# Column quarters over accumulated input tiles in the later modulation, and forward transforms from even and odd times, in a diffusion block on one NeuronCore

## The reference, cut to what matters

```
mx = (silu(c) @ ada_w[i] + ada_b[i])          # 6 * 1024 numbers for each layer
sh1x, sc1x, g1x, sh2x, sc2x, g2x = split(mx, 6)

def _fft_conv(u, kern, skip):
    y = irfft(rfft(u, n=512) * rfft(kern)); return y[:, :256] + u * skip
z = x1 * _fft_conv(v, kern[:, 0], skip[0])
y = x2 * _fft_conv(z, kern[:, 1], skip[1])
```

## Time and profile before

| | us |
|---|---|
| median of 3 runs (lowest, highest) | 1964.73 (1961.82, 1973.62) |
| profiled execution, its own time | 1960.14 |
| its span | 1958.2 |
| PE busy | 1776.7 (91% of the span) |
| DVE busy | 773.4 (39%) |
| ACT busy | 531.2 (27%) |
| mean granted clock of TensorE | 0.969 of full speed |

### The profile page before, as it was taken

How to read it: one execution, slowest core, us unless ns; L and a number is a source line. 1 busy time by engine, 2 the same in 40 slices (tenths; PEclk the granted TensorE clock), 3 DMA queues, 4 the chain that set the end, 5 groups by cost and what they waited for, 6 DMA issues and landing times. The chain is left out here.

```text
span 1958.2 us, 34257 instructions
## 1 busy us (share of the span) xinstructions
PE 1776.7 (91%) x13979; PEld 941.9 (48%) x13979; DVE 773.4 (39%) x1910; ACT 531.2 (27%) x993; POOL 52.1 (3%) x45
## 2 busy tenths in 40 slices
PE   5788898898897888999999999898999999999996
PEld 2344555555555544443443443675654444444442
DVE  5766677777777335200100101564735110110101
ACT  3244454554454321111111111213321111111111
POOL 0010000000100000000000001000000000000001
PEclk8989899999999899999999999999999999999998
DMA  9013323323323468999999997232166999999993
GB/s 308 26 33 101 99 73 114 114 77 111 110 76 127 162 238 360 427 428 428 428 429 428 428 416 277 76 128 112 82 272 272 427 428 428 428 428 428 428 413 123
DMA packets 105168, 504.05 MB, mean 257 GB/s; under 512 B 15568, under 2 KB 60352, under 8 KB 79184
## 3 DMA queue, kind: packets, MB, share of 16 engines
q1 hardware_dynamic: 103728, 501.88, 64.4%
q10 hardware_dynamic: 1312, 0.37, 0.1%
HBM read 501.13 MB, written 1.09 MB: 256 GB/s over the span
## 5 line engine op out<-in xcount | busy, mean ns | idle before, releaser
L2009 DVE TENSOR_TENSOR arena<-banks,arena 128x512 f32<-128x512 f32 x32 | 22.1, 692 | 660.5 <-PE banks L1821 660.5
L1821 PE MATMUL banks<-arena 128*64 128x512 f32 x1024 | 226.4, 594 | 10.5 <-DMA arena<-in_moe_w_up 10.5
L1843 PE MATMUL banks<-arena 128*64 128x512 f32 x1024 | 226.8, 596 | 3.3 <-ACT arena L1940 3.3
L1812 PE MATMUL banks<-arena 128*64 128x512 f32 x1024 | 225.3, 593 | 3.3 <-DVE arena L1932 3.3
L775 PE MATMUL banks<-arena 128*128 128x512 f32 (+1 forms) x384 | 159.3, 553 | 0.8 <-ACT arena L1086 0.8
L1821 PEld LDWEIGHTS banks<-arena 128*64 128x64 f32 x1024 | 82.1, 137 | 152.8 <-issue 152.8
L1812 PEld LDWEIGHTS banks<-arena 128*64 128x64 f32 x1024 | 74.2, 137 | 147.8 <-issue 144.2
L1843 PEld LDWEIGHTS banks<-arena 128*64 128x64 f32 x1024 | 70.7, 137 | 154.4 <-issue 150.7
L1934 ACT ACTIVATE arena<-banks,arena 128x128 f32<-128x128 f32 x128 | 48.1, 456 | 335.5 <-PE banks L1801 335.5
L1801 PEld LDWEIGHTS banks<-arena 128*128 128x128 f32 x1024 | 118.4, 194 | 28.1 <-issue 24.3
L1801 PE MATMUL banks<-arena 128*128 128x128 f32 x1024 | 124.5, 281 | 3.5 <-DVE arena L2004 3.5
(11 more groups left out here) (394 smaller groups left out, 2398.0 us busy)
## 6 DMA issues: line engine op xcount, KB each, us to landing
arena<-in_moe_w_gate SPq DMA_DIRECT2D x64, 2048.0 KB, 14.9
arena<-in_moe_w_up SPq DMA_DIRECT2D x64, 2048.0 KB, 17.1
arena<-in_moe_w_down SPq DMA_DIRECT2D x64, 2048.0 KB, 12.8
arena<-in_ada_w SPq DMA_DIRECT2D x128, 192.0 KB, 2.9
arena<-in_ada_w SPq DMA_DIRECT2D x64, 256.0 KB, 3.5
arena<-in_rw_wrkv SPq DMA_DIRECT2D x24, 512.0 KB, 5.1
arena<-in_hy_w_in SPq DMA_DIRECT2D x6, 2048.0 KB, 8.4
arena<-in_ada_w SPq DMA_DIRECT2D x8, 1024.0 KB, 17.0
```

Of the source, the lines that this page charges most:

```text
L1812: mm = pe.matmul(G[j * CAP:(j + 1) * CAP, :], xT[:, t, j * CAP:(j + 1) * CAP], wg[par][j][:, t], start=(t == 0), stop=(t == KT - 1))
L1821: mm = pe.matmul(U[j * CAP:(j + 1) * CAP, :], xT[:, t, j * CAP:(j + 1) * CAP], wu[j][:, t], start=(t == 0), stop=(t == KT - 1))
L1843: mm = pe.matmul(bank[j * CAP:(j + 1) * CAP, :], hT[:, t, j * CAP:(j + 1) * CAP], wd[j][:, t, half * 512:(half + 1) * 512], start=(t == 0) ...
L2009: dve.tensor_tensor(h, U[:, :], sg, ALU.mult).then_inc(h_ready, 1)
```

## The change

It has two parts.

**Later modulation.** A step now cuts the columns into four quarters (128 or 96 columns, `part`). Each 32-partition quarter of the bank takes one quarter of the columns, and the four input tiles are accumulated in PSUM: 16 matmuls in place of four. No sum across quarters is needed: `total`, its matmul, its bank uses `t0` to `t2`, its ACT copy and its ACT-issued DMA go. DVE's additions are as wide as a quarter; the second one writes `row` directly, after a wait for the row's last DMA. SP issues the store (`store`), ahead of the next piece's bias and weights. The bias is loaded as four rows.

**Convolutions.** Each of the four products of one transform becomes one product without accumulation: even times and odd times, real and imaginary, four matmuls in place of eight. ACT copies the two even ones to `half_even`, which lies in the old `half_b`. DVE forms sum and difference, two instructions for each part, and then multiplies as before, with `half_a` used twice and a drain more. ACT waits for `imag_ready` of the half before.

```
@@ LaterModulation
+    def part(self, piece):
+        return self.width(piece) // 4
+    def store(self, sp, m, piece, open_dve):
+        layer, cols = self.place(m, piece)
+        sp.wait_ge(open_dve, OPEN.taken(m, f"h{2 * piece + 1}")[1])
+        sp.dma_start(self.mods[layer, 0, cols].rearrange("(g n) -> g n", g=4),
+                     self.row[0:P:32, 0:self.part(piece)]).then_inc(self.row_out, 16)
@@ load
             sp.wait_ge(open_done, OPEN.done(*before))
-            if half == 0:
-                sp.wait_ge(open_dve, OPEN.taken(*before)[1])
         if half == 0:
-            sp.dma_start(self.bias[0:1, 0:self.width(piece)], ...)
+            if m or k:
+                self.store(sp, *((m, piece - 1) if piece else (m - 1, self.PIECES - 1)), open_dve)
+            sp.dma_start(self.bias[0:P:32, 0:self.part(piece)], ...)
@@ products
-        for g in range(self.HALF):
-            mm = pe.matmul(bank[g * 32:(g + 1) * 32, 0:self.width(piece)], self.cond[:, half * self.HALF + g],
-                           self.w[g][:, 0:self.width(piece)], start=True, stop=True, tile_position=(0, g * 32))
+        n = self.part(piece)
+        for t in range(self.HALF):
+            for g in range(4):
+                mm = pe.matmul(bank[g * 32:(g + 1) * 32, 0:n], self.cond[:, half * self.HALF + t],
+                               self.w[t][:, g * n:(g + 1) * n], start=(t == 0), stop=(t == self.HALF - 1), tile_position=(0, g * 32))
-    def total(self, pe, m, piece, bank): ...
@@ open_order
-        order += [(m, u) for u in ("h1", "t0") if chain]
+        order += [(m, u) for u in ("h1",) if chain]
-        order += [(m, u) for u in ("t1",) if chain]
-        order += [(m, u) for u in ("t2",) if chain]
@@ rwkv_heads, SP, after the rounds
+            later.store(sp, CH - 1, later.PIECES - 1, open_dve)
@@ rwkv_heads, PE and ACT: total(m, 0), total(m, 1), total(m, 2) removed; ACT's last wait for row_out removed
@@ rwkv_heads, DVE, modulate
+                dve.drain()
                 if later_half:
-                    dve.drain()
-                    dve.tensor_tensor(later.acc[:, 0:width], bank[:, 0:width], later.acc[:, 0:width], ALU.add)
+                    if m or piece:
+                        dve.wait_ge(later.row_out, 16 * (later.PIECES * m + piece))
+                    dve.tensor_tensor(later.row[:, 0:n], bank[:, 0:n], later.acc[:, 0:n], ALU.add)
                 else:
-                    if m or piece:
-                        dve.wait_ge(open_done, OPEN.done(*((m, f"t{piece - 1}") if piece else (m - 1, "t2"))))
@@ hyena_convolutions, PE
-                    for n in range(4):
-                        part, ft = n // 2, n % 2
+                    for part in range(2):
                         if od or half:
-                            pe.wait_ge(vhat_ready, (od * 2 + half) * 4 + n - 3)
+                            pe.wait_ge(vhat_ready, (od * 2 + half - 1) * 2 + part + 1)
                         for i in range(TT):
-                            mm = pe.matmul(s.psum[4 + n][:, :], fwd[part][:, i, ft * P:(ft + 1) * P], vt[...], start=(i == 0), stop=(i == TT - 1))
-                        mm.then_inc(dft_done, 1)
+                            pe.matmul(s.psum[4 + part * 2 + i][:, :], fwd[part][:, i, 0:P], vt[...], start=True, stop=True).then_inc(dft_done, 1)
@@ hyena_convolutions, ACT
-                        act.activation(vhat[:, part, ft, c], s.psum[4 + n][:, :], ACT.Copy).then_inc(vhat_ready, 1)
+                    for part in range(2):
+                        act.wait_ge(dft_done, (od * 2 + half) * 4 + part * 2 + 1)
+                        if od or half:
+                            act.wait_ge(imag_ready, od * 2 + half)
+                        act.activation(half_even[part], s.psum[4 + part * 2][:, :], ACT.Copy).then_inc(half_ready, 1)
@@ hyena_convolutions, DVE
+                    for part in range(2):
+                        dve.wait_ge(half_ready, (od * 2 + half) * 2 + part + 1)
+                        dve.wait_ge(dft_done, (od * 2 + half) * 4 + part * 2 + 2)
+                        a, b = half_even[part], s.psum[5 + part * 2][:, :]
+                        dve.tensor_tensor(vhat[:, part, 0, c], a, b, ALU.add)
+                        first, second = ((a, b), (b, a))[part]
+                        dve.tensor_tensor(vhat[:, part, 1, c], first, second, ALU.subtract).then_inc(vhat_ready, 1)
+                    dve.drain()
...
                     dve.tensor_tensor(prod[:, 1, :, c], vhat[:, 0, :, c], khat[:, od, 1, :, c], ALU.mult)
-                    dve.tensor_tensor(half_b, vhat[:, 1, :, c], khat[:, od, 0, :, c], ALU.mult)
                     dve.drain()
-                    dve.tensor_tensor(prod[:, 1, :, c], prod[:, 1, :, c], half_b, ALU.add).then_inc(imag_ready, 1)
+                    dve.tensor_tensor(half_a, vhat[:, 1, :, c], khat[:, od, 0, :, c], ALU.mult)
+                    dve.drain()
+                    dve.tensor_tensor(prod[:, 1, :, c], prod[:, 1, :, c], half_a, ALU.add).then_inc(imag_ready, 1)
```

More of the change, by code:

```diff
@@ L206, in __init__ @@
         self.w = [s.take(512) for _ in range(self.HALF)]
-        self.acc, self.bias, self.row = s.take(512), s.take(512), s.take(512)
+        self.acc, self.bias, self.row = s.take(P), s.take(P), s.take(P)
         self.w_in, self.bias_in, self.row_out = (s.sem(n) for n in ("later_w_in", "later_b_in", "later_out"))
@@ L798, in modulate @@
                 later.products(pe, m, k, open_bank(m, f"h{k}")).then_inc(open_done, 1)
-            def total(m, piece):
-                bank = open_bank(m, f"t{piece}")
-                pe.wait_ge(open_dve, OPEN.taken(m, f"h{2 * piece + 1}")[1])
-                later.total(pe, m, piece, bank).then_inc(open_done, 1)
             def sum_directions(n):
@@ L1006, in _ @@
                     if chain and slot == 8:
-                        total(m, 0)
                         level_two(m, 1)
@@ L1026, in _ @@
                         from_values_early(n)
-                    if chain and slot == 15:
-                        total(m, 1)
                     if early and 15 <= slot < 18:
@@ L1054, in _ @@
                         level_two(n, 0)
-                    if chain and slot == 23:
-                        total(m, 2)
                     if m == CH - 1 and slot >= 9:
@@ L1187, in chain_solve @@
                 act.activation(U, s.psum[7][:, 0:P], ACT.Copy).then_inc(us_ready, 1)
-            def total(m, piece):
-                width = later.width(piece)
-                bank = read(m, f"t{piece}")
-                if m or piece:
-                    act.wait_ge(later.row_out, 16 * (later.PIECES * m + piece))
-                act.activation(later.row[0:1, 0:width], bank[0:1, 0:width], ACT.Copy).then_inc(open_act, 1)
-                act.wait_ge(open_act, OPEN.taken(m, f"t{piece}")[1])
-                layer, cols = later.place(m, piece)
-                act.dma_start(mods[layer, 0, cols].unsqueeze(0), later.row[0:1, 0:width]).then_inc(later.row_out, 16)
             for m in ROUNDS:
@@ L1261, in _ @@
                         level_two(n, 0)
-                    if chain and slot == 23:
-                        total(m, 2)
-            act.wait_ge(later.row_out, CH * later.PIECES * 16)
         @block.vector
```

26 lines of the change are left out of this document (10 added, 16 removed).

## The result

| | before | after |
|---|---|---|
| median of 4 runs each (lowest, highest) | 1967.86 (1961.82, 1973.62) | 1943.36 (1939.95, 1946.65) |
| ratio to before, 95% interval | | 0.9883 [0.9858, 0.9909] |
| profiled execution, own time | 1960.14 | 1943.53 |
| its span | 1958.2 | 1941.3 |
| mean granted clock | 0.969 | 0.963 |

The ratio is worth 23.0 us (18 to 28). The changed kernel was timed a second time, beside other runs: 0.9910 [0.9886, 0.9934], 17.7 us. The change gains about 20 us where 26.2 were forecast, at the lower edge of the forecast's 20 to 32; the forecast of 1936 is 7 us low.

What follows compares the result with a forecast made beforehand. PE was taken as the bound, busy for 91% of the span, with gaps from DVE and weight waits. Heads 22.7 plus convolutions 3.5 gave 26.2 us, so 1936 us, range 1923 to 1950.

Steps and rivals of the forecast that it cites:

- rounds above 71 us: Heads: a sign that the prediction is wrong would be rounds staying above 71 us; rounds near 69 were expected.
- The totals: Heads: 24 totals taken off PE, 0.95 us for each first and 0.74 for each other, 19.4 us altogether.
- the key projection: Heads, between h3 and L775: total removed and DVE's reading of h3 earlier, 1.26 us gained, at worst 0.74.
- The quarter products: Heads, 48 steps of L239: 32 short records instead of eight, no change taken; at worst 0.43 us a step, 21 us.
- The rival built on that estimate: Heads' quarter steps: records are paid one by one, time about 1957, by the page's reading 1963; chance 0.06.
- the one of groups that follow one another: Heads, L239: the four groups don't stand abreast, steps cost 96 us more, time 2030; chance 0.04.
- The sum of the heads: Heads: 3.05 us in each of rounds 0 to 5, 2.4 in round 6, 2.0 in round 7, together 22.7 us.
- My rival of 0.11: Heads: the clock takes gain back, three more rounds pay 4.0 us each; gain 14, time about 1948; chance 0.11.
- The narrow additions: Heads, DVE: h0's shorter addition gives 0.1 us a round; those of h2 and h3 end h3's reading 0.54 us earlier.
- The convolutions: Convolutions: 2.9 us less in the second order, 2.5 in the first, 5.4 together; 3.5 taken, bounds -1 and 7.
- The loss to half clock: Convolutions: a slow transform back behind the new 3.4 us gap costs 1.3 us in each order, 2.6, leaving 2.8.
- The stores on SP: Heads: 24 stores moved to SP, about 0.24 us each to issue, covered, nothing; uncovered 12 us, a rival of 0.03.

Runs made afterwards that it cites:

- mod_only: Kernel before with only the later-modulation part of the change: 1947.45 us, ratio 0.9936 to the kernel before.
- no_totals: Kernel before without the totals, keeping wide products and additions, stores on SP, sum over the four input tiles left out: 1944.09 us, ratio 0.9923.
- no_reload: Changed kernel without loads for each piece's second half; h1, h3, h5 reuse the tiles of h0, h2, h4 (wrong values): 1920.78 us, ratio 0.9779.
- best_b: Changed kernel with the edits of warm_after and even_free, two unused matmuls in the convolutions' gap, h5 at the end of slot 23: 1926.07 us, ratio 0.9810.
- h15_later: Changed kernel with h1 moved from slot 6 to 7 and h5 from slot 21 to the end of slot 23: 1938.60 us, ratio 0.9893.
- warm_before: Kernel before with two unused matmuls a round in the gap ahead of the chain's third step: 1957.82 us, ratio 0.9964.
- conv_only: Kernel before with only the convolutions' part of the change: 1961.42 us, ratio 0.9984 to the kernel before.
- warm_after: Changed kernel with two unused matmuls a round in the gap ahead of the chain's third step: 1934.64 us, ratio 0.9864 to the kernel before.
- after_again: Changed kernel run once more, unedited, in the second group: 1946.70 us, ratio 0.9910 to the kernel before.
- even_free: Changed kernel with half 1's even parts copied into unread columns of vt, without ACT's wait for imag_ready: 1945.87 us, ratio 0.9906.

## Why the prediction was right, and where a size was off

The time fell into the range, and the mechanism, removed sums on PE, is the one that gave it. One of the signs that I had named for being wrong is there all the same: rounds above 71 us, five of six in the changed kernel's first execution and two of six in mod_only. It points at the heads.

**The totals.** No L246 is left. The terms showed where they were put (1.21 us at the key projection for 1.26; a round at full clock 69.1 to 69.8 us for about 69). no_totals shows that leaving them out is enough for the gain of the heads.

**The quarter products** cost nothing, as taken from the 64 records in 1.16 us: 1.08 and 0.87 us. The 29 us of loss that I had estimated from the Trainium skill (TensorEngine Tiling (Array Packing), Instruction Overhead), with its 60 cycles laid on top of the streaming, aren't there: with 96 and 128 columns in a record and four groups side by side the step hardly changed. The rival built on that estimate, and the one of groups that follow one another, are refuted by the same rows. (By the step that put the forecast at 1936, that rival's time would have been 1965, not 1963.)

**The sum of the heads is the step that was mis-sized**: 22.7 us were put on the end of the heads, and mod_only measured 12.6 (8 to 17). I had written that "in most rounds h1 already waits for its weights" and counted nothing for it. That says only that an earlier arrival there is lost; the terms ahead of h1 and h5 should then not have been summed in full. In rounds 0 to 5 the forecast's terms sum to 18.3 us; the executions give 13.1 in the mean, with 3.9 us more of waiting for weights, and 13.8 with 3.7 more where the clock is held up in both kernels. So by their size the waits are most of the shortfall there; that they cost whole microseconds no_reload shows. Counted as a term, some 4 us, they would have put the whole gain at 22. I had read all 15 waits as h1's and h5's; one of h3 and one of h4 are among them. There the loads with all that hangs on them are worth 24.7 us in seven rounds, and best_b shows that 7 to 11 of them can be had by a place for h5. My rival of 0.11, in which the clock takes the gain back, isn't shown in this sum. What else is missing between 22.7 and 12.6 stays open; the interval of mod_only reaches 4 us to either side.

**The narrow additions** (0.1 us and 0.54 a round, 3 to 4 us in all) end sooner as counted, and nothing that the runs can tell follows from it: behind the key projection PE waits longer for ACT, at h5 for a DMA.

**The convolutions.** Measured 3.1 us (0.6 to 5.7) for the forecast 3.5, which lies between 5.4 without the clock's price and 2.8 with it. From first transpose to output product the traces give 2.6 to 2.8 us where the first transposes run at the same clock: 64.44 (before, mod_only) against 61.84 (h15_later) at full clock, and 65.16 (no_totals, warm_before) against 62.35 to 62.57 at half clock. With the gap filled it is 4.9 (64.44 to 59.5). So by the traces the price was paid in full, and the lower figure, 2.8, was the right one. The second order ended 26.9 us after its transform's start (1377.99 to 1404.89), 26.7 forecast, with a gap of 3.24 us for 3.4, DVE being the bound. The loss to half clock was put at 1.3 us in each order, 2.6 in all. It is 2.5 to 2.8 in all in each of the six executions with this gap, but divided otherwise: 2.6 to 2.8 and none in four of them (after, conv_only, h15_later, warm_after), 1.1 and 1.4 in two (after_again, no_reload). The way to the 1.3 wasn't right for the first four, as a transform back was taken to lose at most 1.7 us (5.2 for 3.5); that the sum fits is in part luck. The Trainium skill (TensorE: Matmul & The Clock Gate, HAM oscillation), by which each burst after a gap starts cold, agrees with both orders of after_again (8.55 and 8.86 us) and with the first of after (10.06), not with its second (7.46).

**The stores on SP** take 0.51 to 0.57 us to issue, not 0.24, and neither h2 nor h4 waits for weights in the changed kernel. In the last round h4's wait of 0.26 us is gone.

**What the traces alone don't tell.** At the first transpose of the convolutions the changed kernel is 13.2 us ahead (1342.54 against 1355.70), at the end of the heads 9.3 (711.36 against 720.68). The 3.8 us between come from stages that the change doesn't touch. Two profiled executions can't weigh a change of 1%; the interleaved runs can.

**Open.** Why the same kernel behind the same gap of 3.24 us loses 2.6 us in the first order and none in the second in one execution, and 1.1 and 1.4 in another. How large the clock's part of the missing gain is: 2 to 4 us by the whole times, less than 1 by rounds 0 to 5, all within the noise. Whether the kernel before would gain as much from no_reload: it wasn't run. How much of the loads' 24.7 us is landing time and how much the half clock behind it, beyond the 17.9 us of waits and the 8.1 us of PE's busy time, which overlap.

## What to carry to other kernels

Before summing removed work over a chain, list the waits for transfers along it whose start moves with the chain's own steps: in front of each, an earlier arrival is lost unless the consumer is moved back too, and moving one product (h5) was worth 7 to 10 us, a third to a half as much as the whole change. Count a gap on PE with the speed of what follows it; in a gap that DVE makes, two unused matmuls a round gave back 7 to 12 us. Before a difference of a few us between two traces is explained, look at other executions of the same code: the same heads differed by 8 us. A sum over partition groups is best avoided by giving each group other columns: 32 short matmuls in four groups cost what 8 long ones did.

## What the runs showed of the hardware

- The 32 weight loads and 32 matmul records of a quarter step run in 1.08 us for 128 columns and 0.87 for 96; cutting columns four times finer cost 0.01 to 0.02 us a step (1.07 and 0.85 before).
- A gap of 3.24 us on PE was followed by half clock (1.2 in place of 2.4 GHz) for part of a transform in the first order (10.06 us for 7.46) and by full clock in the second, in one execution of the changed kernel, and by shorter stretches of half clock in both orders (8.55, 8.86) in another. A gap of 2.67 us gave 8.71 and 8.86. In the heads a gap of 2.57 us and a weight wait of 0.4 to 1.0 behind it are followed by either (1.08 us in round 1, 1.94 in round 3).
- Added work shortened the time: two unused matmuls a round, 7.7 us before and 12.1 after by medians (7.1 and 9.0 by the ratios).
- The same loads behind the same product let h1 start 7.0 to 7.7 us after h0 within one execution (even_free, rounds 0 to 7); without the loads it comes at 6.41 in five of the first six rounds.
